# Folding the token transform of a 2-D Fourier mixing branch by its even and odd symmetry

## The reference

```
F_GROUPS = 4
F_GROUP_W = 64
def fourier_mix(u):                       # u: (1, 512, 256)
    b_, l_, _ = u.shape
    g = u.astype(jnp.float32).reshape(b_, l_, F_GROUPS, F_GROUP_W)
    y = jnp.real(jnp.fft.fft2(g, axes=(1, 3), norm='ortho'))
    return y.reshape(b_, l_, -1).astype(u.dtype)
```

## Time and profile before

| | us |
|---|---|
| time, median of 3 runs | 956.63 (955.57 to 956.84) |
| profiled execution: its own time | 955.41 |
| profiled execution: span from first to last instruction | 953.6 |
| TensorE busy | 886.0 (93% of the span) |
| VectorE / ScalarE / GpSimd busy | 389.8 / 196.9 / 105.2 |
| mean DMA rate | 153 GB/s |

### The profile page before, as it was taken

The page is one execution under the profiler, slowest core; times in us unless marked ns, Lnnn a source line. Parts: engine busy times, 40 slices in busy tenths (PEclk is TensorE's granted clock), DMA queues, the critical chain, the costliest instruction groups (busy, mean ns, idle before and its releaser), DMA issues.

```text
span 953.6 us, 9781 instructions
## 1 busy us (share of the span) xinstructions
PE 886.0 (93%) x3795; PEld 459.3 (48%) x3795; DVE 389.8 (41%) x801; ACT 196.9 (21%) x430; POOL 105.2 (11%) x98
## 2 busy tenths in 40 slices
PE   5999999999999999999999999999993999999970
PEld 1345465755754445555555555444552444444430
DVE  0366254654335225665576651101337422222224
ACT  0510165200011023232232220010121111112200
POOL 0000000000147300011100111110001000000003
PEclk9999999999999999999999999999995999999995
DMA  8941120300081106153242536204043499999717
GB/s 317 333 161 43 47 89 1 111 1 1 2 308 38 73 8 229 54 184 101 90 156 89 197 110 243 89 0 155 22 145 124 155 359 366 369 366 369 281 68 265
DMA packets 80862, 145.77 MB, mean 153 GB/s; under 512 B 5344, under 2 KB 38320, under 8 KB 80816
## 3 DMA queue, kind: packets, MB, share of 16 engines
q1 hardware_dynamic: 75056, 124.18, 37.8%
q0 software_dynamic: 3456, 12.58, 3.6%
q10 hardware_dynamic: 2304, 8.39, 2.2%
HBM read 132.55 MB, written 12.58 MB: 152 GB/s over the span
## 4 chain that ended last, share of the span: by engine, by line
PE 88%; DMA 4%; DVE 2%; SPq 2%; ACT 1%; issue 1%; POOL 1%; POOLq 0%; DVEq 0%; PEldq 0%
PE ps L462 84%; PE ps L465 5%; DMA arena<-in_w_in 2%; DMA arena<-ye,slot_of 1%; DMA arena<-in_mod_w 1%; SPq L377 1%; POOL arena L1676 1%; ACT arena L934 1%; DMA arena<-xd,tok_of 0%; SPq L371 0%; DMA ye<-arena 0%; DVE arena L1523 0%; POOLq L101 0%; DVE arena L1207 0%; ACT arena L1121 0%
## 5 line engine op out<-in xcount | busy, mean ns | idle before, releaser
L462 PE MATMUL ps<-arena 128*128 128x512 f32 (+8 forms) x2910 | 768.5, 446 | 11.7 <-DVE arena L1462 5.7
L462 PEld LDWEIGHTS ps<-arena 128*128 128x128 f32 (+4 forms) x2910 | 362.1, 169 | 373.9 <-issue 354.3
L934 ACT ACTIVATE arena<-ps 128x128 f32<-128x128 f32 (+2 forms) x133 | 56.1, 445 | 190.4 <-PE ps L462 143.5
L1326 DVE SCALAR_TENSOR_TENSOR arena<-arena,ps 128x512 f32<-128x512 f32 x32 | 22.0, 687 | 131.1 <-ACT arena L1024 130.9
L465 PEld LDWEIGHTS ps<-tab,arena 128*128 128x128 f32 (+1 forms) x492 | 56.6, 144 | 36.2 <-issue 29.1
L465 PE MATMUL ps<-tab,arena 128*128 128x128 f32 (+1 forms) x492 | 65.6, 275 | 8.0 <-DMA arena<-xd,tok_of 3.3
L1647 POOL TENSOR_TENSOR arena<-arena 128x512 f32<-128x512 f32 x24 | 30.4, 1265 | 279.9 <-DVE arena L1326 279.9
L1024 ACT ACTIVATE arena<-ps 128x512 f32<-128x512 f32 x32 | 19.1, 598 | 198.7 <-PE ps L462 198.7
L1612 POOL TENSOR_TENSOR stat<-stat,mhalf 128x12 f32<-128x12 f32 (+3 forms) x17 | 22.0, 1294 | 340.6 <-DVE stat L1162 340.4
L1562 DVE TENSOR_TENSOR arena<-arena,ps 128x256 f32<-128x256 f32 x16 | 6.7, 421 | 96.9 <-ACT arena L1131 96.9
L1294 DVE SCALAR_TENSOR_TENSOR arena<-arena,cond 128x512 f32<-128x512 f32 x56 | 42.6, 760 | 2.3 <-PE ps L465 0.6
(11 more groups left out here) (150 smaller groups left out, 384.8 us busy)
## 6 DMA issues: line engine op xcount, KB each, us to landing
arena<-in_moe_w SPq DMA_DIRECT2D x32, 1024.0 KB, 9.4
arena<-in_w_in SPq DMA_DIRECT2D x13, 2048.0 KB, 10.6
arena<-in_mod_w SPq DMA_DIRECT2D x16, 1024.0 KB, 5.2
arena<-in_moe_w SPq DMA_DIRECT2D x32, 512.0 KB, 10.8
arena<-in_mod_w SPq DMA_DIRECT2D x4, 2048.0 KB, 12.3
ye<-arena ACTq DMA_DIRECT2D x16, 512.0 KB, 7.6
arena<-in_w_out SPq DMA_DIRECT2D x2, 2048.0 KB, 8.5
arena<-in_x SPq DMA_DIRECT2D x4, 512.0 KB, 12.6
```

What stands on the lines that cost most here:

```text
L462: return nc.tensor.matmul(o, l, r, start=start, stop=stop, skip_group_check=True)
L934: return A_(o, i, ACT.Copy)
L1326: V.scalar_tensor_tensor(merged[:, half * 4 + j, :] if g < 8 else gtmp[:, g % 2, :], th[:, g % 2, :], 1.0, ps[:, gate_bank(g)[0] + 1, :], ...
```

## The change

The token transform is folded. cos(2 pi s t / 512) is the same for token s and token 512-s, the sine has the opposite sign. So for s = 1 to 255 the sum fu[s] + fu[512-s] can stand in for both tokens in the cosine part and the difference fu[s] - fu[512-s] in the sine part. VectorE makes them (`fold`); token 0 is copied into both, and token 256 has a cosine part only (`gcM`, `dftM`: stationary and moving operand of one partition). In the same way output t and output 512-t share the cosine sum (even part) and have opposite sine sums (odd part): TensorE makes both parts for t = 0 to 256 only, 257 columns, in a bank each; ScalarE copies the even part to `eL`, and VectorE writes even + odd to outputs 0 to 256 and even - odd, from back to front, to outputs 511 to 257 (`unfold`). The table is loaded for 257 rows and 257 columns alone, in three DMAs.

```diff
@@ sync
             sp.wait_ge(yG_ready, XT)
-            sp.dma_start(dftL, A["dft_long"].rearrange("c (s p) t -> p c s t", p=P)).then_inc(dft_in, 16)
+            for c in range(2):
+                sp.dma_start(dftL[:, c], A["dft_long"][c, 0:HALF, 0:HALF + 1].rearrange("(s p) t -> p s t", p=P)).then_inc(dft_in, 16)
+            sp.dma_start(dftM[0:1, :], A["dft_long"][0, HALF:HALF + 1, 0:HALF + 1]).then_inc(dft_in, 16)
@@ tensor
-            for t in range(XT):
-                if t >= 2:
-                    pe.wait_ge(gcs_ready, t - 1)
+            pe.wait_ge(fold_ready, 1)
+            for s in range(2):
                 for ft in range(2):
-                    last = mm(ps[:, 2 + 2 * (t % 2), ft * 256:(ft + 1) * 256], fuT[:, ft, t * P:(t + 1) * P],
-                              tab[:, DFT:DFT + 256], True, True)
+                    for c in range(2):
+                        last = mm(ps[:, 2 + 2 * s, ft * 256 + c * P:ft * 256 + (c + 1) * P], fold[:, ft, c, s * P:(s + 1) * P],
+                                  tab[:, DFT + c * P:DFT + (c + 1) * P], True, True)
+                if s == 0:
+                    for ft in range(2):
+                        last = mm(ps[0:1, 3, ft * P:(ft + 1) * P], fuT[:, ft, HALF:HALF + 1], tab[:, DFT:DFT + P], True, True)
                 last.then_inc(fgc_done, 1)
-            pe.wait_ge(gcs_ready, XT)
-            pe.wait_ge(dft_in, 16)
+            pe.wait_ge(gcs_ready, 2)
+            pe.wait_ge(dft_in, 48)
             for ft in range(2):
-                for s in range(XT):
-                    for c in range(2):
-                        last = mm(ps[:, 2 + 2 * ft, :], gcs[:, s, ft * 256 + c * P:ft * 256 + (c + 1) * P],
-                                  dftL[:, c, s, :], s == 0 and c == 0, s == XT - 1 and c == 1)
+                for s in range(2):
+                    mm(ps[:, 2 + 2 * ft, 0:HALF + 1], gcs[:, s, ft * 256:ft * 256 + P], dftL[:, 0, s, :], s == 0, False)
+                mm(ps[:, 2 + 2 * ft, 0:HALF + 1], gcM[0:1, ft, :], dftM[0:1, :], False, True)
+                for s in range(2):
+                    last = mm(ps[:, 3 + 2 * ft, 0:HALF + 1], gcs[:, s, ft * 256 + P:(ft + 1) * 256], dftL[:, 1, s, :], s == 0, s == 1)
                 last.then_inc(yF_done, 1)
@@ scalar
-            for t in range(XT):
-                act.wait_ge(fgc_done, t + 1)
-                copy(gcs[:, t, :], ps[:, 2 + 2 * (t % 2), :]).then_inc(gcs_ready, 1)
+            for s in range(2):
+                act.wait_ge(fgc_done, s + 1)
+                if s == 0:
+                    copy(gcM[0:1].rearrange("p a n -> p (a n)"), ps[0:1, 3, 0:2 * P])
+                copy(gcs[:, s, :], ps[:, 2 + 2 * s, :]).then_inc(gcs_ready, 1)
             for ft in range(2):
                 act.wait_ge(yF_done, ft + 1)
-                copy(yT[:, 1, ft, :], ps[:, 2 + 2 * ft, :]).then_inc(yF_ready, 1)
+                copy(eL[:, ft, :], ps[:, 2 + 2 * ft, 0:HALF + 1]).then_inc(eL_ready, 1)
@@ vector
             dve.wait_ge(yG_ready, XT)
+            dve.wait_ge(pj_done, 26)
+            for ft in range(2):
+                front, back = fuT[:, ft, 1:HALF], fuT[:, ft, SEQ - 1:HALF:-1]
+                V.tensor_copy(fold[:, ft, :, 0:1], fuT[:, ft:ft + 1, 0:1].broadcast_to([P, 2, 1]))
+                V.tensor_tensor(fold[:, ft, 0, 1:HALF], front, back, ALU.add)
+                last = V.tensor_tensor(fold[:, ft, 1, 1:HALF], front, back, ALU.subtract)
+            last.then_inc(fold_ready, 1)
+
+            def unfold(ft):
+
+                dve.wait_ge(eL_ready, ft + 1)
+                odd = ps[:, 3 + 2 * ft, :]
+                V.tensor_tensor(yT[:, 1, ft, 0:HALF + 1], eL[:, ft, :], odd[:, 0:HALF + 1], ALU.add)
+                V.tensor_tensor(yT[:, 1, ft, SEQ - 1:HALF:-1], eL[:, ft, 1:HALF], odd[:, 1:HALF], ALU.subtract).then_inc(yF_ready, 1)
+
             for t in range(7):
...
                 gated(t)
+                if t == 3:
+                    for ft in range(2):
+                        unfold(ft)
```

More of the change, by code:

```diff
@@ L185, in build @@
         PT = region(R1 + 1536, 2, 768)
-        dftL = region(R1, 2, XT, SEQ)
-        gcs = region(R1 + 4096, XT, 512)
+        HALF = SEQ // 2
+        dftL = region(R1, 2, 2, HALF + 1)
+        dftM = region(R1 + 1280, HALF + 1)
+        eL = region(R1 + 1600, 2, HALF + 1)
+        gcM = region(R1 + 3584, 2, P)
+        gcs = region(R1 + 4096, 2, 512)
+        fold = region(R1 + 5120, 2, 2, HALF)
         merged = region(R_G + 6656, KD, SEQ)
@@ L248, in build @@
         att_done, attm_ready, o_done, o_read, yG_ready = sem("att_done"), sem("attm_ready"), sem("o_done"), sem("o_read"), sem("yG_ready")
-        fgc_done, gcs_ready, yF_done, yF_ready = sem("fgc_done"), sem("gcs_ready"), sem("yF_done"), sem("yF_ready")
+        fold_ready, fgc_done, gcs_ready = sem("fold_ready"), sem("fgc_done"), sem("gcs_ready")
+        yF_done, eL_ready, yF_ready = sem("yF_done"), sem("eL_ready"), sem("yF_ready")
         qk_norm, rope_done = sem("qk_norm"), sem("rope_done")
```

## The result

The changed kernel takes **946.57 us** (median of 4 runs, 944.85 to 948.2) against 956.57 us before (median of 4, 955.57 to 956.84): ratio 0.9896, 95% interval 0.988 to 0.9912, so 10.0 us less. 946.0 was forecast, between 943.9 and 948.6. The profiled execution has a span of 943.5 us and took 945.3 us, against 953.6 and 955.41 before.

A forecast was written before the change was run, and what follows sets the result against it. TensorE, busy 93% of the span, was taken to bound the kernel. Stage 2's -9.42 us and stage 1's -1.17 us make -10.59 us, from a median of 956.63 to 946.0 us; range 943.9 to 948.6 with 8 in 10.

The forecast's parts named there:

- What bounds the kernel: Whole kernel: TensorE, busy 93% of the span, sets the end, so time taken out of stage 2 comes off it.
- Stage 2: TensorE's second transform stage: ten matmuls of 257 columns at 0.431 us take 4.31 us instead of 13.73; term -9.42 us.
- the two with one partition counted in full: Stage 2: its two one-partition matmuls were priced like the other eight, at 0.431 us each.
- Stage 1: First transform stage, TensorE and ScalarE's copies: 20 passes at 0.116 us, then copies; term -1.17 us, from -1.6 to +0.3.
- The estimate drawn from the page of the Trainium skill: Stage 1: the four single-row passes would load almost for free, taking some 0.2 us off the sum.
- The fold: VectorE behind the recurrence's output: six instructions, 2.1 to 2.6 us, covered by 39 us, so no cost on the path.
- The queue behind the unfold: VectorE's norms 4 and 5 and `gated(4)` after the unfold: 9.2 us to spare before TensorE asks, so no cost.
- rival that VectorE's queue becomes the path: Four unfolding instructions delay norms 4 and 5: at 2.7 us each slack is gone, at 6 us each 959; chance 0.02.
- The clock rival: Thinner stage 1, with a 1 us wait, lowers TensorE's clock: a loss of 2.3 to 3.3 us, about 949; chance 0.04.
- The range: Whole kernel's time: 943.9 to 948.6 us with 8 in 10, from stage 1's price, run spread and clock.

The follow-up runs named there:

- e1: The change with only the outputs folded: stage 1 as before the change, 16 matmuls of 257 columns in stage 2; 948.22 us, ratio 0.9923.
- e2: The change with only the inputs folded: stage 2 has 10 matmuls of 512 columns and there is no unfold; 949.52 us, ratio 0.9938.
- e9: The changed kernel run once more, unaltered, on the same chip; 947.82 us, ratio 0.9903.
- e3: The change without the two one-partition matmuls of stage 2, so token 256 is missing from the outputs; 945.5 us (one run).
- e4: The change with the two one-partition matmuls of stage 2 placed next to each other; 945.65 us (one run).
- e5: The change with the one-partition matmuls of stage 2 padded to 128 partitions; 944.95 us, ratio 0.9885.
- e6: The change with eight unused dependent VectorE instructions, 7.9 us in all, right behind the unfold; 946.71 us.
- e7: The change with 18 unused dependent VectorE instructions, 17.8 us in all, right behind the unfold; 954.65 us, ratio 0.9988.
- e8: The change with one-partition matmuls padded to 128 partitions, and stage 1 and its copies moved ahead of gate 3; 942.4 us, ratio 0.9862.
- e10: The change with only stage 1 and its copies moved ahead of gate 3, one-partition matmuls unpadded; 944.39 us, ratio 0.9878.
- e11: The kernel of e8 run once more, beside e9; 942.64 us, ratio 0.9858.

## Why the prediction was right

**What bounds the kernel** was read rightly: e1 and e2 move the time by TensorE's columns, and the whole of what the stretch lost (9.66 us) reached the end. Own times: 955.41 - 945.3 = 10.1 us. The transposes start 9.57 us earlier (the stretch less 0.09 us by which it began later), the remaining 0.5 us lie behind them, and no edit here accounts for them. That the median came within 0.6 us of the forecast is partly luck: the four executions stand in two pairs, 944.85 and 945.3 at a mean clock of 0.971, 947.84 and 948.2 at 0.969 and 0.967, and the median is the middle of a gap in which none of them lies; the six of e9 have 947.82. What the traces bear out is 9.66 us of the 10.59.

**Stage 2** was priced at 4.31 us and measured 5.11. The price of 257 columns was right (e1: 0.435 us a matmul against 0.431). The step that was mis-sized is "the two with one partition counted in full": they cost 0.82 us each, not 0.43, for the passage between 128 partitions and 1. e3, e4 and e5 show that with three different edits. The term is -8.62 us instead of -9.42, and from stage 1's start to gate 4 it takes 8.54 us, where 7.6 were forecast.

**Stage 1** was -1.17 and is 3.43 - 4.47 = -1.04 us. The first twelve loads last the forecast 1.39 us; behind the four single-row passes there is a gap of 0.23 us, so that the 20 loads take 308.57 - 305.99 = 2.58 us instead of 2.32. Stage 1 as a whole is 0.13 us longer than worked out. The estimate drawn from the page of the Trainium skill, some 0.2 us less for the single-row passes, did not come.

**The fold** was put at 2.1 to 2.6 us and took 1.5. Operands read or written backwards cost what forward ones do, 0.41 to 0.43 us for 255 to 257 elements, and such instructions follow each other 0.33 us apart, so that the sum of their lengths is too much. It was covered as foretold.

**The queue behind the unfold.** VectorE was through with it at 316.04, 0.9 us later than worked out, since stage 2 took 0.8 us longer, for the reason above. The slack of 9.2 us is what the trace has, and e6 and e7 show both sides of it: 7.9 us are hidden, of 17.8 us 7.05 come through. The rival that VectorE's queue becomes the path was thus rightly conditioned, and far off: the four unfolding instructions take 0.41 to 0.43 us each, where it needed 2.7.

**The clock rival.** Stage 1, with its wait of under 1 us, kept 1.00. e7 shows such a fall 30 us further on, 0.85 us behind a wait of 2.17 us.

**The range.** Half of it stood for the clock and for the spread of the runs, and it was needed: 944.85 to 948.2 in four runs of one kernel.

## What to carry to other kernels

Where TensorE is busy without a gap and the chain runs through it, count columns and passes: halving the width of a float32 matmul to 257 columns halved its time, and the additions that pay for it are free as long as the other engine's queue has slack, which can be read from where it next has to be done. Don't let a leftover row be a matmul of its own with one partition: pad it to the shape of its neighbours (0.77 us here, for two such matmuls). And small edits are judged by a stretch of the trace that the clock does not touch; medians of four runs moved by more than these edits were worth.

## What the runs showed of the hardware

**The passage from 128 partitions to 1 and back costs 0.39 us**, at 257 columns (the change) as at 512 (e2), once per visit and not per matmul (e4), and not at all with the operand padded to 128 (e5).

**The clock falls in one execution and not in another, at the same place of the same program.** From 257 to 264 us TensorE runs small matmuls of the recurrence and is busy throughout. The window of the profiled execution of the change:

```profile
257.00:264.00 7.00, 7.00 (x86) 5.68 (x81) 2.52 (x7) 0.00 (x0) 1.01 (x1) 0.76 0.01 2
```

Of the same kernel in e9_change_again:

```profile
257.00:264.00 7.00, 7.00 (x96) 5.98 (x96) 2.48 (x8) 0.38 (x1) 1.01 (x1) 1.00 0.01 2
```

Before the change it was 0.76 too, so the two profiles that the result compares are alike in this. In the change's trace the lower level lasts from 260.3 to 263.7 us; half speed for these 3.4 us of work is, as an estimate, 1.7 us lost. Behind it, where TensorE mostly waits for the routing of tokens to experts, from 690 to 745 us, the change:

```profile
690.00:745.00 55.00, 36.11 (x203) 22.41 (x202) 30.92 (x98) 9.45 (x22) 5.77 (x7) 0.75 0.49 163
```

And e9_change_again:

```profile
690.00:745.00 55.00, 36.30 (x196) 24.19 (x196) 28.89 (x86) 9.44 (x22) 5.75 (x7) 0.69 0.48 163
```

The mean clock of 0.75 or 0.69 goes with 603.1 or 606.3 us from the transposes to the end: e1, e2, e8, e10 and e11 have 0.72 to 0.75 and 603.1 to 603.8 us, e3 to e6 have 0.69 and 605.2 to 605.7. That is as large as the spread of some 3 us between executions of one kernel. The mean granted clock is on record for every execution, traced or not, and the times go with it: e10's four at 0.972 took 944.02 to 944.43 us, its two at 0.969 took 945.77 and 945.99. The Trainium skill, "TensorE: Matmul & The Clock Gate", section on HAM oscillation, has such falls come from gaps between bursts. e7 agrees. The falls near 700 us begin ahead of the long waits: in e9 TensorE was busy for 3.25 of the last 4.70 us before. At 257 us TensorE was busy for 7.00 of 7.00 us, and for all of the 22 us before, so there it was no gap; whether it was the small matmuls, no run shows.

Whether e8 and e11, both with a narrow spread around 942.5, hit the shorter fall because their timing suits it, or by chance, stays open. The mean clock was 0.971 or more in 10 of the 15 executions with stage 1 early (e8, e10, e11), in 2 of the 10 of the change, and in 14 of the 30 of before that ran beside the experiments. It is not all of the difference either: at 0.969 the six of e9 have a median of 947.82 us, and the two of e11 took 943.16 and 943.91. So of the 5.2 us between e9 and e11 only 1.57 are shown to be the edits'.
